# Two paddings move the stationary buffers of an fp32r encoder kernel within 1024 bytes

## The chip, the cores and the metric

The kernel runs on one core of one Trainium2 chip. The metric is the device time of one execution in microseconds (us). Before the change three runs gave 2340.24, 2340.43 and 2341.03 us; the median is 2340.43.

## The reference

One layer of an encoder over 256 tokens of width 2048, in float32. What is computed:

```
x = x + 0.5 * (silu(n1 @ w_gate) * (n1 @ w_up)) @ w_down        # n1 = rms_norm(x), width 5632
h = rms_norm(x);  u = h @ w_in                                  # conv, gate, latents, two merge gates
y_conv = silu(layer_norm(depthwise_conv_31(a * sigmoid(gate)))) @ w_pw_out
y_mla  = attention(16 heads, q from a latent of 768, k and v from a latent of 512, rotary 64) @ w_o
x = x + (sigmoid(gl_conv) * y_conv + sigmoid(gl_mla) * y_mla) @ w_out
x = x + 0.5 * (silu(n2 @ w_gate) * (n2 @ w_up)) @ w_down        # n2 = rms_norm(x), the second feed-forward
return rms_norm(x)
```

All products have float32 operands; the kernel keeps float32 precision by splitting each operand into a high and a low fp32r part and adding three products.

## The kernel before

**Tiling.** The contraction dimension lies on the 128 partitions in tiles of 128 (KT = 16 for width 2048, FT = 44 for 5632, QT = 6, KVT = 4 for the latents). A weight matrix is streamed in units: two contraction tiles of 512 columns each (`DEEP` = 2, `WIDE` = 512), 512 KB. SyncE loads each unit into `raw`, ScalarE rounds it into `w_hi` (L431), VectorE takes the rest into `w_lo` (L926). All three are rings of four slots of 4096 bytes per partition; slot `u % 4` is reused once TensorE has counted unit `u` in `unit_used`.

**TensorE.** `wide_unit` (L770) waits for `lo_ready`, and for both contraction tiles and both halves of the tokens calls `multiply` (L678), which issues three matmuls: at L681 high by high, at L682 high by low, at L683 low by high. So a unit has 12 matmuls. Activations are the stationary operand (128 by 128, loaded by a weight load of its own, PEld in the profile), the streamed weights are the moving one (128 by 512). Which buffer is stationary depends on the stage (`STATIONARY`, L732): `h` for both up/gate stages, conv_in, the latents, the two merge gates and conv_out; `hidden` for both down-projections; `attn` for mla_out; `merged` for w_out; `c_q` for q_rope. In the trace a matmul is named bank<-moving,stationary. The heads (`head_pair`, L833) use products of 256 columns: with the weight block stationary and `c_q` or `c_kv` moving, and for the values with `c_kv` stationary and the weights moving. Scores, probabilities and values are plain float32 matmuls from `q_nope`, `k_nope`, `q_rope`, `probs_t` and `value`.

**Layout of a stationary buffer.** `hidden` is [128, 44, 2, 256] fp32r: per contraction tile 1024 bytes of high parts and 1024 bytes of low parts, each of two halves of 512 bytes (128 tokens). `h`, `attn` and `merged` have the same form with 16 tiles, `c_q` with 6, `c_kv` with 4. A weight slot is 2 x 2048 bytes. So every operand of these matmuls begins a multiple of 512 bytes behind the start of its buffer.

**Places in SBUF.** Buffers are laid one behind the other in the order of their `sb(...)` calls (L172), each rounded up to 32 bytes; members of one `outs` stack share a start. Byte addresses within a partition and their remainders by 1024:

| buffer | address | mod 1024 |
|---|---|---|
| raw, w_hi, w_lo | 1152, 17536, 33920 | 128 |
| x | 50304 | 128 |
| h | 66688 | 128 |
| identity | 99456 | 128 |
| prod (also probs, angle), opened (also probs_t) | 104608, 108704 | 160 |
| before_hidden | 112800 | 160 |
| hidden, padded (they share a start; padded is 18304 bytes) | 112832 | 192 |
| q_rope, attn, merged (they share a start) | 131136 | 64 |
| sig_conv, sig_mla, conv_tok | 163904, 180288, 196672 | 64 |
| c_kv, c_q | 196672, 204864 | 64 |
| k_rope, q_nope, k_nope, value | 217152 to 223296 | 64 |

The last buffer ends at 227392. `before_hidden` is itself a padding that nothing reads or writes.

**Order of the work.** ffn1_up (22 groups of 8 units), ffn1_down (4 groups of 22), conv_in, latents, conv_gate, mla_gate, q_rope, heads, mla_out, conv_out, w_out, ffn2_up, ffn2_down. While conv_in to the heads run, the 31-tap depthwise convolution is made beside them by ScalarE (L539: padded times a tap into q_rope) and VectorE (L1116: sum within q_rope, L1122: padded times a tap plus q_rope). After most groups TensorE turns a result by transposes (L692), which ScalarE (L493) and VectorE (L1058) put into `hidden` or `merged` as high and low parts.

Of the kernel before, what the change touches and what calls it, by code (L numbers as in the profile page):

```python
# [14 lines left out]
P = 128  # L15
# [148 lines left out]
def encoder(nc, streams, xt_in, x_in, pos_in, gains_in, final_in, taps_in, const_in, freq_in, out):  # L164
# [6 lines left out]
    with ExitStack() as ctx:  # L171
        def sb(name, shape, dt=F32, stack=ctx):  # L172
            return stack.enter_context(nc.sbuf_tensor(name, shape, dt))
# [41 lines left out]
        active = prod[:, :, :].rearrange("p a (b t) -> p (a b) t", b=2)  # L215

        sb("before_hidden", [P, 8])

# [9 lines left out]

        padded = sb("padded", [P, KT, T + 2 * PAD])
        conv = padded[:, :, PAD:PAD + T]
        outs = ExitStack()
        attn = sb("attn", [P, KT, 2, T], F32R, outs)
        outs.close()
# [1114 lines left out]
```

## Time and profile before

| | |
|---|---|
| median of three runs | 2340.43 us |
| the profiled execution's own time | 2340.69 us |
| its span, first to last instruction | 2338.9 us |
| TensorE busy | 2312.5 us, 99% |
| VectorE busy | 1322.0 us, 57% |
| ScalarE busy | 1188.5 us, 51% |
| DMA, share of 16 engines | 60.3% |
| granted TensorE clock | 0.998 of full speed |

Matmuls are pipelined, so the length of one in the trace (390 ns for 512 columns) is longer than the distance from its start to the next one's start. Busy time is the union of these spans. What a matmul costs in the stream is read from starts: the start of a late one minus the start of an early one, over the number of steps between them. This distance is called the pitch below. An n-row timeline that shows the first and the last matmul has n - 1 steps.

### The profile page before, as it was taken

To read this page: it belongs to the slowest core of one execution; us is meant where nothing else is said; L and a number is where in the kernel's file an instruction comes from. 1 tells how busy PE (TensorE), PEld (TensorE's weight loads), DVE (VectorE), ACT (ScalarE), POOL (GpSimd) and SP (SyncE) were. 2 spreads that over 40 slices of the span, in tenths; PEclk is the share of its full clock that TensorE was granted. 3 is DMA by queue.
4 is the path that set the end of the run, shared out by engine and by line. 5 is a ranking of instruction groups with operands and counts; after the bars stand their busy time and mean duration, and the time that the engine had idled before them with its cause. 6 is when DMAs were issued, how large, how long until landed. Compare 5 with 4: busy or idle time off the path is not lost.

```text
span 2338.9 us, 26788 instructions
## 1 busy us (share of the span) xinstructions
PE 2312.5 (99%) x10718; PEld 1923.4 (82%) x10718; DVE 1322.0 (57%) x1470; ACT 1188.5 (51%) x1620; POOL 0.2 (0%) x4
## 2 busy tenths in 40 slices
PE   8999999999999999999999999999999999999997
PEld 7888888888888888878889888888888888888886
DVE  5545544544545488997875465555544544544443
ACT  6444444444444577787776564444444444443343
POOL 0000000000000000000000000000000000000000
PEclk9999999999999999999999999999999999999999
DMA  8666666665656666566643456666666666666664
GB/s 287 188 189 192 187 189 191 188 188 188 183 187 183 194 190 183 178 193 186 196 139 116 144 172 188 185 185 207 189 187 191 189 187 192 188 188 189 188 188 128
DMA packets 121532, 432.65 MB, mean 185 GB/s; under 512 B 13632, under 2 KB 13888, under 8 KB 121280
## 3 DMA queue, kind: packets, MB, share of 16 engines
q1 hardware_dynamic: 121408, 430.93, 60.3%
q8 instruction: 85, 1.39, 0.3%
q14 instruction: 39, 0.32, 0.0%
HBM read 428.78 MB, written 2.10 MB: 184 GB/s over the span
## 4 chain that ended last, share of the span: by engine, by line
PE 97%; DVE 1%; ACT 1%; issue 1%; DMA 0%; SPq 0%; ACTq 0%; DVEq 0%
PE bank L681 31%; PE bank L683 31%; PE bank L682 31%; PE turned L692 2%; PE bank L824 1%; PE bank L798 1%; PE bank L799 1%; DVE q_rope L1116 0%; PE turned L809 0%; ACT w_hi L431 0%; DVE w_lo L926 0%; DVE q_rope L1122 0%; DMA raw<-in_ffn_up 0%; PE turned L878 0%; ACT q_rope L539 0%
## 5 line engine op out<-in xcount | busy, mean ns | idle before, releaser
L926 DVE TENSOR_TENSOR w_lo<-raw,w_hi 128x1024 fp32r<-128x1024 f32 (+2 forms) x814 | 986.6, 1215 | 967.8 <-ACT w_hi L431 967.5
L431 ACT ACTIVATE w_hi<-raw 128x1024 fp32r<-128x1024 f32 (+2 forms) x814 | 853.3, 1052 | 1011.4 <-PE bank L683 1004.8
L681 PE MATMUL bank<-w_hi,h 128*128 128x512 f32 (+1 forms) x2144 | 836.0, 390 | 10.3 <-DVE w_lo L926 10.3
L683 PE MATMUL bank<-w_hi,h 128*128 128x512 f32 (+1 forms) x2144 | 832.9, 388 | 0.0
L682 PE MATMUL bank<-w_lo,h 128*128 128x512 f32 (+1 forms) x2144 | 832.8, 388 | 0.0
L681 PEld LDWEIGHTS bank<-w_hi,h 128*128 128x128 f32 x2144 | 403.2, 188 | 93.3 <-DVE w_lo L926 11.6
L683 PEld LDWEIGHTS bank<-w_hi,h 128*128 128x128 f32 x2144 | 403.0, 188 | 82.9
L682 PEld LDWEIGHTS bank<-w_lo,h 128*128 128x128 f32 x2144 | 403.3, 188 | 81.4
L681 PE MATMUL bank<-w_hi,hidden 128*128 128x512 f32 x704 | 278.9, 396 | 0.0
L682 PE MATMUL bank<-w_lo,hidden 128*128 128x512 f32 x704 | 278.4, 395 | 0.0
L683 PE MATMUL bank<-w_hi,hidden 128*128 128x512 f32 x704 | 278.4, 395 | 0.0
L683 PEld LDWEIGHTS bank<-w_hi,hidden 128*128 128x128 f32 x704 | 132.4, 188 | 32.0
L682 PEld LDWEIGHTS bank<-w_lo,hidden 128*128 128x128 f32 x704 | 132.4, 188 | 31.7
L681 PEld LDWEIGHTS bank<-w_hi,hidden 128*128 128x128 f32 x704 | 132.4, 188 | 31.6
L539 ACT ACTIVATE q_rope<-padded,taps 128x256 f32<-128x256 f32 x320 | 135.8, 498 | 1.0 <-DVE q_rope L1116 1.0
L1116 DVE TENSOR_TENSOR q_rope<-q_rope 128x1024 f32<-128x1024 f32 x76 | 92.5, 1217 | 0.0
L1122 DVE SCALAR_TENSOR_TENSOR q_rope<-padded,taps,q_rope 128x256 f32<-128x256 f32 x160 | 66.6, 477 | 0.0
L681 PE MATMUL bank<-w_hi,attn 128*128 128x512 f32 x128 | 52.4, 410 | 0.0
L458 ACT ACTIVATE opened<-bank,rstd 128x512 f32<-128x512 f32 x52 | 33.0, 685 | 37.4 <-PE bank L683 37.4
L681 PE MATMUL bank<-w_hi,merged 128*128 128x512 f32 x128 | 50.6, 395 | 0.0
L683 PE MATMUL bank<-w_hi,merged 128*128 128x512 f32 x128 | 50.2, 392 | 0.0
L683 PE MATMUL bank<-w_hi,attn 128*128 128x512 f32 x128 | 50.2, 392 | 0.0
(171 smaller groups left out, 1219.3 us busy)
## 6 DMA issues: line engine op xcount, KB each, us to landing
raw<-in_ffn_up SPq DMA_DIRECT2D x352, 512.0 KB, 4.0
raw<-in_ffn_down SPq DMA_DIRECT2D x176, 512.0 KB, 3.7
raw<-in_conv_in SPq DMA_DIRECT2D x64, 512.0 KB, 3.8
raw<-in_conv_gate SPq DMA_DIRECT2D x32, 512.0 KB, 4.1
raw<-in_mla_gate SPq DMA_DIRECT2D x32, 512.0 KB, 4.1
raw<-in_mla_out SPq DMA_DIRECT2D x32, 512.0 KB, 3.6
raw<-in_conv_out SPq DMA_DIRECT2D x32, 512.0 KB, 3.6
raw<-in_w_out SPq DMA_DIRECT2D x32, 512.0 KB, 3.6
```

The lines of the kernel that those rows point to most:

```text
L431: act.activation(w_hi[:, j, 0:n], raw[:, j, 0:n], ACT.Copy).then_inc(hi_ready, 1)
L458: act.activation(opened[:, tt, :], banks(g)[tt][:, :], func, scale=rstd[:, tt:tt + 1]).then_inc(by_act, 1)
L539: act.activation(conv_prod[made % 2][:, r, :], padded[:, m, t:t + T], ACT.Copy, scale=taps[:, m, t:t + 1]).then_inc(tap_made, 1)
L681: pe.matmul(dst, fixed_hi, moving_hi, start=first, stop=False)
L682: pe.matmul(dst, fixed_hi, moving_lo, start=False, stop=False)
L683: return pe.matmul(dst, fixed_lo, moving_hi, start=False, stop=last)
L692: last = pe.transpose(turned_bank[n % 2][:, r * T + tt * P:r * T + (tt + 1) * P], src[:, tt, c:c + P], identity[:, :])
L798: pe.matmul(dst, q_nope[:, j, cols], k_nope[:, j, :], start=True, stop=False)
L799: last = pe.matmul(dst, q_rope[:, p, 0, cols], k_rope[:, j, :], start=False, stop=True)
L926: dve.tensor_tensor(w_lo[:, j, 0:n], raw[:, j, 0:n], w_hi[:, j, 0:n], ALU.subtract).then_inc(lo_ready, 1)
L1116: dve.tensor_tensor(dst, conv_acc, conv_prod[made % 2], ALU.add).then_inc(tap_done, 1)
L1122: dve.scalar_tensor_tensor(out=conv_acc[:, r, :], in0=padded[:, m, t:t + T], scalar=taps[:, m, t:t + 1], in1=conv_acc[:, r, :], op0=ALU.mu ...
```

## The change

`before_hidden` grows from 8 to 248 float32 values per partition (32 to 992 bytes), and a new padding `before_attn` of 32 values (128 bytes) is put between `padded` and the buffers that begin with `attn`, `q_rope` and `merged`. Neither is read or written. No instruction, wait, size, shape or order of the kernel changes.

```diff
@@ -215,7 +215,7 @@
-        sb("before_hidden", [P, 8])
+        sb("before_hidden", [P, 248])
@@ -231,6 +231,7 @@
         padded = sb("padded", [P, KT, T + 2 * PAD])
         conv = padded[:, :, PAD:PAD + T]
+        sb("before_attn", [P, 32])
         outs = ExitStack()
         attn = sb("attn", [P, KT, 2, T], F32R, outs)
```

By the rule above `hidden`, `padded`, `xt`, `x0_squares` and `final_gain` move up by 960 bytes, and `attn`, `q_rope`, `merged` and all that lies behind them by 960 + 128 = 1088 bytes. `hidden` then begins at 113792 (128 mod 1024), `attn` and `merged` at 132224 (128), `c_kv` at 197760 (128), `c_q` at 205952 (128). The last buffer ends at 228480.

## Rows read from the trace of the kernel before

**Rows 1.** The page: busy us of each engine; the granted clock in tenths.

```profile
PE 2312.5 (99%) x10718; PEld 1923.4 (82%) x10718; DVE 1322.0 (57%) x1470; ACT 1188.5 (51%) x1620; POOL 0.2 (0%) x4
...
PEclk9999999999999999999999999999999999999999
```

**Rows 2.** The page: the chain that ended last, by engine.

```profile
PE 97%; DVE 1%; ACT 1%; issue 1%; DMA 0%; SPq 0%; ACTq 0%; DVEq 0%
```

**Rows 3.** Timeline of PE: start us, length us, operation; stationary h, 90 rows.

```profile
1139.67 0.39 PE L682 MATMUL bank<-w_lo,h 128*128 128x512 f32 x1
...
1159.84 0.39 PE L681 MATMUL bank<-w_hi,h 128*128 128x512 f32 x1
```

**Rows 4.** Timeline of PE, the second down-projection, 86 rows.

```profile
2119.98 0.39 PE L682 MATMUL bank<-w_lo,hidden 128*128 128x512 f32 x1
...
2139.81 0.40 PE L683 MATMUL bank<-w_hi,hidden 128*128 128x512 f32 x1
```

**Rows 5.** Timeline of PE, w_out with stationary merged, 49 rows.

```profile
1532.90 0.39 PE L681 MATMUL bank<-w_hi,merged 128*128 128x512 f32 x1
...
1543.88 0.39 PE L681 MATMUL bank<-w_hi,merged 128*128 128x512 f32 x1
```

**Rows 6.** Timeline of PE, q_rope stage with stationary c_q, 50 rows.

```profile
1165.75 0.39 PE L683 MATMUL bank<-w_hi,c_q 128*128 128x512 f32 x1
...
1176.96 0.39 PE L681 MATMUL bank<-w_hi,c_q 128*128 128x512 f32 x1
```

**Rows 7.** Groups of PE by form: count, busy us, mean ns, idle before.

```profile
L682 PE MATMUL bank<-w_lo,hidden 128*128 128x512 f32 x704 | 278.4, 395 | 0.0
...
L682 PE MATMUL bank<-w_lo,merged 128*128 128x512 f32 x128 | 49.8, 389 | 0.0
L682 PE MATMUL bank<-w_lo,attn 128*128 128x512 f32 x128 | 49.8, 389 | 0.0
...
L682 PE MATMUL bank<-w_lo,c_q 128*128 128x512 f32 x24 | 9.4, 393 | 0.0
```

**Rows 8.** Timeline of DVE during the first down-projection, 17 rows.

```profile
515.17 1.23 DVE L926 TENSOR_TENSOR w_lo<-raw,w_hi 128x1024 fp32r<-128x1024 f32 x1 [1.57 <-ACT w_hi L431]
...
559.97 1.23 DVE L926 TENSOR_TENSOR w_lo<-raw,w_hi 128x1024 fp32r<-128x1024 f32 x1 [1.57 <-ACT w_hi L431]
```

**Rows 9.** Groups of PE by form: short products of the heads.

```profile
L682 PE MATMUL bank<-c_q,w_hi 128*128 128x256 f32 x96 | 26.8, 279 | 0.0
...
L682 PE MATMUL bank<-c_kv,w_hi 128*128 128x256 f32 x64 | 18.0, 281 | 0.0
```

**Rows 10.** Timeline of PE, heads, c_kv moving, then stationary, 24 rows.

```profile
1219.93 0.28 PE L682 MATMUL bank<-c_kv,w_hi 128*128 128x256 f32 x1
...
1222.65 0.28 PE L681 MATMUL bank<-w_hi,c_kv 128*128 128x256 f32 x1
```

**Rows 11.** Timeline of PE, heads, c_q moving, 12 rows.

```profile
1245.60 0.28 PE L683 MATMUL bank<-c_q,w_lo 128*128 128x256 f32 x1
...
1246.85 0.28 PE L682 MATMUL bank<-c_q,w_hi 128*128 128x256 f32 x1
```

**Rows 12.** Timeline of PE, 320 columns with stationary h, 18 rows.

```profile
971.98 0.30 PE L681 MATMUL bank<-w_hi,h 128*128 128x320 f32 x1
...
974.47 0.31 PE L683 MATMUL bank<-w_hi,h 128*128 128x320 f32 x1
```

**Rows 13.** Groups of DVE, 820:1070: count, busy us, mean ns, idle before, releaser.

```profile
L926 DVE TENSOR_TENSOR w_lo<-raw,w_hi 128x1024 fp32r<-128x1024 f32 (+1 forms) x93 | 109.6, 1185 | 30.7 <-ACT w_hi L431 30.6
L1116 DVE TENSOR_TENSOR q_rope<-q_rope 128x1024 f32<-128x1024 f32 x49 | 59.6, 1217 | 0.0
L1122 DVE SCALAR_TENSOR_TENSOR q_rope<-padded,taps,q_rope 128x256 f32<-128x256 f32 x103 | 42.9, 477 | 0.0
```

**Rows 14.** Waits: engine and line, releaser, us in total, times, longest.

```profile
ACT w_hi L431 <- PE bank L683: 1004.8, 635, 2.2
...
PE bank L681 <- DVE w_lo L926: 10.3, 4, 8.4
```

## The prediction

> **What bounds the kernel now.** I read the page first: TensorE is busy 99% of the span at full granted clock in every slice [rows 1], and the chain that ended last is TensorE for 97% [rows 2]. The waits say the same from the other side: ScalarE waits 1004.8 us in all for TensorE to give back a ring slot, while TensorE waits 10.3 us for weights [rows 14]. So only two things can move the time: the number of matmuls, which the change leaves alone, and what one costs in the stream. The engines that feed it have room.
>
> That cost is read next, from starts in the timeline, stage by stage. With stationary `h`: 90 rows from 1139.67 to 1159.84, so 20.17 us over 89 steps = 226.6 ns a matmul [rows 3]. With stationary `hidden`: 86 rows, 19.83 us over 85 steps = 233.3 ns [rows 4]. The first down-projection has the same pitch, seen from VectorE, which splits one unit of weights per 12 matmuls: 44.80 us over 16 steps = 2.800 us, and 2.800 / 12 = 233.3 ns [rows 8]. With stationary `merged`: 10.98 us over 48 steps = 228.8 ns [rows 5]. With stationary `c_q`: 11.21 us over 49 steps = 228.8 ns [rows 6]. These are the same 512 columns, the same moving buffers and the same three-product pattern; 512 columns at 2.4 GHz, the granted level, are 213.3 ns, so `h` pays 13.3 ns on top, `merged` and `c_q` 15.5, `hidden` 20.0.
>
> **What the difference goes with.** By the table of places, `w_hi`, `w_lo` and `h` stand at 128 in 1024 bytes; `merged` and `c_q` at 64; `hidden` at 192. Equal place has the lowest pitch; two buffers at 64 have one pitch though they lie 73 KB apart. I tried three other readings against this. It is not how far up in SBUF the buffer lies: `hidden` covers 112832 to 202944, which contains `merged`, and `c_q` lies above it all, yet both are cheaper. It is not the neighbours' work: VectorE is idle 1.57 us of each 2.80 us unit in the down-projection [rows 8], and in the w_out stage the other engines do the same weight work. It is not a wait, because a wait would show as a few long steps, and here the whole stream is slower. What the trace can't separate is place relative to the weights from place as such; after the change both are those of `h`, so the forecast does not need it. The chunks within a buffer begin at multiples of 512 bytes in all of them, so nothing within it spoils the equality. What the equality does not cover are the remainders by 4096 and more; within `h` these run through all values while the pitch stays 226.6, so I take them as without effect.
>
> A rule speaks against the change. The Trainium skill, "TensorE: Matmul & The Clock Gate", in the section on what happens when you issue a matmul, says that TensorE has two independent read ports, so that loading the next weights does not take read bandwidth from the running matmul; it gives 215.7 ns as the distance of warm matmuls of 512 columns. By it no place could matter and the gain would be nil. This case's trace disagrees on the level already: 226.6 to 233.3 ns, at the full clock.
>
> **The change, part by part.** Nothing is added to any queue; no instruction, wait or transfer is moved past another. Only addresses change.
>
> *hidden, 192 to 128.* Three lines of 704 matmuls are 2112 [rows 7]. Each goes from 233.3 to 226.6 ns [rows 3, 4]: 2112 x 6.66 ns = 14.1 us, all on the path, since TensorE is the chain there.
>
> *attn and merged, 64 to 128.* Three lines of 128 for each are 768 [rows 7]. `merged` goes from 228.8 to 226.6 ns [rows 3, 5]; `attn` begins at the same address, and I take its pitch as that of `merged`: 768 x 2.12 ns = 1.6 us.
>
> *c_q as the stationary buffer, 64 to 128.* Three lines of 24 are 72 [rows 7]: 72 x 2.15 ns = 0.2 us [rows 3, 6].
>
> *The short products of the heads.* Here `c_q` moves (3 x 96 products) and `c_kv` moves or is stationary (3 x 64 each way), 672 in all [rows 9], with 256 columns. Before no row shows them at equal place. Their pitch now has two levels: 2.72 us over 23 steps = 118.3 ns [rows 10] and 1.25 us over 11 steps = 113.6 ns [rows 11]. Lower bound of the new cost: all at 113.6 ns, a gain of at most 672 x 4.7 ns = 3.2 us. Upper bound: a short product at equal place is shown with 320 columns and stationary `h`, 2.49 us over 17 steps = 146.5 ns [rows 12]; 320 columns at 2.4 GHz are 133.3 ns, so it pays 13.2 ns, as the long ones do. Carried to 256 columns (106.7 ns) that is 119.9 ns, a loss of at most 672 x 6.3 ns = 4.2 us. The rows nearest in shape are the heads' own, between the two ends; I take 0, and keep -3.2 and +4.2.
>
> *Plain float32 products and transposes* read buffers that also move. They show no effect of place that I can price, and I take 0.
>
> *The other engines.* `padded` and `q_rope`, on which the convolution runs, both come to 128. The sum within `q_rope` takes 1217 ns, all its operands being at one place already [rows 13]; so equal places are no burden to VectorE there. 0, with the far end priced as a rival.
>
> *What is late next.* A unit of the down-projections shrinks from 2.80 to 12 x 226.6 ns = 2.72 us. That is the rate at which ScalarE, VectorE and the loads already feed the `h` stages. VectorE's idle time per unit falls from 1.57 to 1.49 us. If that cover were absent, the 14.1 us would be lost in part, which is the same result as the partial rival below.
>
> Sum: 14.1 + 1.6 + 0.2 + 0 = 15.9 us. Against the profiled execution's own 2340.69 us this is 2324.8; the median of the three runs is 0.26 us lower, so the forecast is 2340.4 - 15.9 = **2324.5 us**, 0.7% less.
>
> **The rivals.**
>
> *A: only part of it goes away.* `hidden` differs from `h` also in its depth of 44 tiles and in the remainders by larger powers of two. If it falls only to the 228.8 ns that `merged` and `c_q` have, and they stay, the gain is 2112 x 4.5 ns = 9.6 us: 2330.8 us. For it: these are the only other values seen. Against it: the pitch is flat in both down-projections, whatever the tile [rows 4, 8].
>
> *B: place is not the cause*, and the paddings do nothing, by the rule of ports or because the stage sets the pitch in a way I haven't seen: 2340.4 us. For it: in the trace place and buffer always go together, so this is a correlation over four buffers. Against it: `merged` and `c_q`, in different stages and of different depth, agree to 0.1 ns.
>
> *C: slower, through the convolution.* Now that `padded`, `q_rope` and the rings share one place, VectorE's tap operations could clash. In 820 to 1070 us they are 59.6 + 42.9 = 102.5 us, and VectorE is idle for 30.7 us [rows 13]. Longer by a share g they cost 102.5g - 30.7 once that is positive. To end 4.7 us above the time before, with the 15.9 us saved, 102.5g has to be 51.3, so it decides from g = 0.5 on. At a doubling it is 71.8 us: 2340.4 - 15.9 + 71.8 = 2396.3 us. Against it: 1217 ns within `q_rope`, at one place, beside 1185 ns for the split, at one place too [rows 13].
>
> **How the numbers follow.** Forecast 0.81, A 0.08, B 0.08, C 0.03. The forecast's own range is 2324.5 - 3.2 = 2321.3 to 2324.5 + 4.2 = 2328.7. The range given reaches on to A and leaves out B and C: 2321 to 2332. What a measurement of this kernel can tell from no change is about 0.2%, 4.7 us; so faster is the forecast and A, 0.89; the same is B, 0.08; slower is C, 0.03.
>
> **What would show it.** In the changed kernel's timeline the down-projections must have 226.6 ns from start to start and VectorE's splits there a period of 2.72 us; the two down-projections together must be 14 us shorter, half in each. `merged`, `attn` and `c_q` must read 226.6. The `h` stages must not change. The heads tell the open term: 113.6, 118.3 or 119.9 ns. If `hidden` reads 228.8, A holds; if it reads 233.3, B does. If the tap operations are longer than 1217 and 477 ns, C is at work. The prediction would be wrong above all if equal place were good only together with something else that `h` has and `hidden` has not.

## The result and the profile after

The changed kernel took 2326.68 us (median of six runs, 2326.39 to 2327.34) against 2340.67 us for the kernel before beside it: a ratio of 0.9941 with a 95% interval of 0.9929 to 0.9953, or 14.0 us less. The forecast was 15.9 us less; the time lies inside its range of 2321 to 2332 us.

The page of the changed kernel, to be read against [rows 1]:

```profile
span 2324.8 us, 26788 instructions
...
PE 2299.0 (99%) x10718; PEld 1924.4 (83%) x10718; DVE 1322.2 (57%) x1470; ACT 1188.3 (51%) x1620; POOL 0.2 (0%) x4
...
PEclk9999999999999999999999999999999999999999
```

TensorE is busy 99% of the span at full clock as before, with the same 10718 matmuls; its busy time fell by 13.5 us and the span by 14.1. So the matmuls themselves became cheaper. The timeline of TensorE in the second down-projection, the same stretch as [rows 4], first and last of 88 rows:

```profile
2119.96 0.39 PE L683 MATMUL bank<-w_lo,hidden 128*128 128x512 f32 x1
...
2139.68 0.39 PE L683 MATMUL bank<-w_lo,hidden 128*128 128x512 f32 x1
```

19.72 us over 87 steps are 226.7 ns, where 233.3 ns stood before. VectorE's splits in the first down-projection (first and last of 17 rows), against [rows 8]:

```profile
514.10 1.23 DVE L927 TENSOR_TENSOR w_lo<-raw,w_hi 128x1024 fp32r<-128x1024 f32 x1 [1.49 <-ACT w_hi L432]
...
557.62 1.23 DVE L927 TENSOR_TENSOR w_lo<-raw,w_hi 128x1024 fp32r<-128x1024 f32 x1 [1.49 <-ACT w_hi L432]
```

43.52 us over 16 steps are 2.72 us a unit, or 226.7 ns for each of 12 matmuls. The heads show the other sign. A run of their short products, first and last of 17 rows, against [rows 10] and [rows 11]:

```profile
1214.03 0.28 PE L683 MATMUL bank<-w_lo,c_kv 128*128 128x256 f32 x1
...
1215.95 0.29 PE L684 MATMUL bank<-w_hi,c_kv 128*128 128x256 f32 x1
```

1.92 us over 16 steps are 120.0 ns, where 118.3 and 113.6 ns stood in [rows 10] and [rows 11]. Over all steps with `c_q` or `c_kv` (under 200 ns, 628 of them) the mean went from 116.8 to 119.8 ns.

The stages, from the first start to the last one of one line (columns: count, least, median and greatest length in ns, first and last start in us). The kernel before: the two down-projections, the first product of the heads, `attn`, `merged`:

```profile
L681 PE MATMUL bank<-w_hi,hidden x352: 393/398/481, 499.0 to 748.1; 128*128 128x512 f32 x176
...
L681 PE MATMUL bank<-w_hi,hidden x352: 393/396/476, 2078.3 to 2324.8; 128*128 128x512 f32 x176
...
L681 PE MATMUL bank<-c_q,w_hi x96: 276/281/469, 1182.0 to 1298.6; 128*128 128x256 f32 x96
...
L681 PE MATMUL bank<-w_hi,attn x128: 392/394/584, 1308.7 to 1407.7; 128*128 128x512 f32 x128
...
L681 PE MATMUL bank<-w_hi,merged x128: 388/394/477, 1498.2 to 1588.9; 128*128 128x512 f32 x128
```

The changed kernel (L682 is L681 of before, since a line was added above it):

```profile
L682 PE MATMUL bank<-w_hi,hidden x352: 389/389/477, 498.2 to 740.5; 128*128 128x512 f32 x176
...
L682 PE MATMUL bank<-w_hi,hidden x352: 389/389/477, 2071.2 to 2310.8; 128*128 128x512 f32 x176
...
L682 PE MATMUL bank<-c_q,w_hi x96: 277/283/472, 1174.3 to 1292.5; 128*128 128x256 f32 x96
...
L682 PE MATMUL bank<-w_hi,attn x128: 387/389/586, 1302.7 to 1401.4; 128*128 128x512 f32 x128
...
L682 PE MATMUL bank<-w_hi,merged x128: 389/389/476, 1491.9 to 1581.9; 128*128 128x512 f32 x128
```

| stretch | before, us | after, us | difference | forecast |
|---|---|---|---|---|
| first down-projection | 249.1 | 242.3 | -6.8 | -7.0 |
| second down-projection | 246.5 | 239.6 | -6.9 | -7.0 |
| heads | 116.6 | 118.2 | +1.6 | 0 (-3.2 to +4.2) |
| attn | 99.0 | 98.7 | -0.3 | -0.8 |
| merged | 90.7 | 90.0 | -0.7 | -0.8 |

The rows sum to -13.1 us. Of the rest of the span's 14.1 us, 0.8 us had passed already when `hidden` began (499.0 against 498.2 in these rows), in a stage that the change does not touch. That is scatter from run to run: in the twelve profiles in which `h` lies at equal place, `hidden` begins anywhere between 497.8 and 499.3 us. So that much is not credited to the change. (`c_q` as the stationary buffer, not in the table, took 17.13 us from its first to its last start before and 17.00 after.)

### The profile page after: what moved, and what is told of

It reads as the page before. It is cut to its first block, busy times and chain, and to the rows that moved or that the text cites. A ratio compares the mean times of both kernels' runs of the same rounds, so it can differ in the third digit from the quotient of the medians.

```text
span 2324.8 us, 26788 instructions
## 1 busy us (share of the span) xinstructions
PE 2299.0 (99%) x10718; PEld 1924.4 (83%) x10718; DVE 1322.2 (57%) x1470; ACT 1188.3 (51%) x1620; POOL 0.2 (0%) x4
## 4 chain that ended last, share of the span: by engine, by line
PE 97%; DVE 1%; ACT 1%; issue 1%; DMA 0%; SPq 0%; ACTq 0%; DVEq 0%
PE bank L682 31%; PE bank L684 31%; PE bank L683 31%; PE turned L693 2%; PE bank L825 1%; PE bank L799 1%; PE bank L800 1%; DVE q_rope L1117 0%; PE turned L810 0%; ACT w_hi L432 0%; DVE w_lo L927 0%; DVE q_rope L1123 0%; DMA raw<-in_ffn_up 0%; PE turned L879 0%; ACT q_rope L540 0%
## 5 line engine op out<-in xcount | busy, mean ns | idle before, releaser
L682 PE MATMUL bank<-w_hi,h 128*128 128x512 f32 (+1 forms) x2144 | 835.9, 390 | 10.1 <-DVE w_lo L927 10.1
L684 PE MATMUL bank<-w_hi,h 128*128 128x512 f32 (+1 forms) x2144 | 832.7, 388 | 0.0
L682 PEld LDWEIGHTS bank<-w_hi,h 128*128 128x128 f32 x2144 | 403.0, 188 | 92.7 <-DVE w_lo L927 11.4
L684 PEld LDWEIGHTS bank<-w_hi,h 128*128 128x128 f32 x2144 | 402.9, 188 | 83.1
L682 PE MATMUL bank<-w_hi,hidden 128*128 128x512 f32 x704 | 274.3, 390 | 0.0
L684 PE MATMUL bank<-w_hi,hidden 128*128 128x512 f32 x704 | 273.9, 389 | 0.0
L684 PEld LDWEIGHTS bank<-w_hi,hidden 128*128 128x128 f32 x704 | 132.1, 188 | 27.5
L682 PEld LDWEIGHTS bank<-w_hi,hidden 128*128 128x128 f32 x704 | 132.1, 188 | 27.4
L1117 DVE TENSOR_TENSOR q_rope<-q_rope 128x1024 f32<-128x1024 f32 x76 | 92.6, 1218 | 0.0
L682 PE MATMUL bank<-w_hi,attn 128*128 128x512 f32 x128 | 52.0, 407 | 0.0
L682 PE MATMUL bank<-w_hi,merged 128*128 128x512 f32 x128 | 50.2, 392 | 0.0
L684 PE MATMUL bank<-w_hi,attn 128*128 128x512 f32 x128 | 50.1, 392 | 0.0
L683 PE MATMUL bank<-w_lo,attn 128*128 128x512 f32 x128 | 49.9, 390 | 0.0
```

What stands on the lines that cost most here:

```text
L682: pe.matmul(dst, fixed_hi, moving_hi, start=first, stop=False)
L683: pe.matmul(dst, fixed_hi, moving_lo, start=False, stop=False)
L684: return pe.matmul(dst, fixed_lo, moving_hi, start=False, stop=last)
L1117: dve.tensor_tensor(dst, conv_acc, conv_prod[made % 2], ALU.add).then_inc(tap_done, 1)
```

## The experiments

All but `e6_hidden_16` differ from the kernel before by paddings alone. A distance below is the place of the stationary buffer less that of the moving one; for products of 512 columns the moving one is a weight ring. As `s1` and the runs behind it show, it counts by its remainder by 256, so 192 means 64 bytes short. To follow the addresses one thing in the rule for places has to be put right: buffers of different `outs` stacks share a start, and those of one stack lie one behind the other, as `probs` and `probs_t` do in the table.

**Each part alone.** `e1_hidden_only` moves `hidden` and puts the buffers behind it back to 64:

```diff
-        sb("before_hidden", [P, 8])
+        sb("before_hidden", [P, 248])
+        sb("before_attn", [P, 16])
```

> Only the feed-forward's buffer moves: hidden to 128 in 1024 bytes, while attn, merged, c_kv and c_q stay at 64. Theory (a buffer's place against the weight rings sets the pitch, and nothing else does): hidden reads 226.6 ns from start to start, merged and c_q stay at 228.8, the short products of the heads stay at 113.6 to 118.3 ns, and the time is 2340.7 - 14.1 = 2326.6 us, the same as with both paddings, since what those lose on attn, merged and c_q here the heads give back. Rival (moving the heads' buffers cost nothing, and hidden brought only the 12.3 us that are left of 14.0 after attn, merged and c_q): 2328.4 us.

Measured: 2326.87 us (2326.63 to 2328.67, five runs), ratio 0.9944 (0.9932 to 0.9957). All steps with stationary `hidden` have a mean of 226.7 ns, those with `merged` and `c_q` 228.9. The first product of the heads in its tile view:

```profile
L682 PE MATMUL bank<-c_q,w_hi x96: 276/281/470, 1175.0 to 1291.6; 128*128 128x256 f32 x96
```

1291.6 - 1175.0 = 116.6 us, the value of before. The forecast's term for `hidden` and the loss in the heads are both as the theory has them. The rival's 2328.4 us is not met by the median, though one of the five runs took 2328.67; what decides against it is that the heads fell back by the 1.6 us. Moving `attn`, `merged`, `c_kv` and `c_q` brought nothing on balance.

`e2_heads_back` keeps both paddings and takes the heads' buffers out of equal place again, together with all that lies behind `merged`:

```diff
+        sb("before_sig_conv", [P, 112])
         sig_conv = sb("sig_conv", [P, 2, D])
```

> Both paddings stay, and a third of 448 bytes ahead of sig_conv puts c_kv and c_q at 576 in 1024, which is 64 in 512. Theory (the place counts by its remainder by 512, since every operand begins a multiple of 512 bytes behind its buffer's start): the short products fall back from 120 ns to the 113.6 to 118.3 of before, the heads take the 126.8 us of before and not 128.4, c_q as the stationary buffer reads 228.8, and the time is 2326.7 - 1.6 + 0.2 = 2325.3 us. Rival (the remainder by 1024 counts, so 576 is a new place): the short products read something else than either. Second rival (the 1.6 us more in the heads are not from their place): 128.4 us and 2326.8 us.

Measured: 2325.08 us (2324.53 to 2326.11), ratio 0.9935 (0.9921 to 0.9948). Its heads:

```profile
L683 PE MATMUL bank<-c_q,w_hi x96: 276/281/469, 1175.1 to 1291.9; 128*128 128x256 f32 x96
```

1291.9 - 1175.1 = 116.8 us, against 118.2 in the changed kernel. (The 126.8 and 128.4 us of the expectation run on to the first product of `attn`.) `c_q` as the stationary buffer reads 228.9 ns, and the mean of the short products is 117.1. So what the heads had lost came from the place of `c_kv` and `c_q`, and a place 512 bytes further on is the same place. The padding moves the operands of the plain float32 products too, but those kept their 215.8 ns. To see whether this version is really ahead of the changed kernel, both ran on one chip, as `e7_change_again` and `e8_heads_back_again`.

> The changed kernel itself once more, beside the next one on one chip: 2326.7 us.

> The changed kernel with the third padding, which puts c_kv and c_q at 64 in 512 again, beside the changed kernel on one chip. Theory (equal place is dearer for products of 256 columns, cheaper for 512): 1.4 to 1.6 us below the changed kernel, 2325.1 us against 2326.7. Rival (the 1.6 us between the two earlier results came from the chip or the hour): no difference between these two.

Measured: 2326.52 us (2326.16 to 2327.08, five runs) for the changed kernel and 2325.36 us (2324.81 to 2325.83, five runs) for the one with the third padding. The two sets of runs do not touch; the difference is 1.2 us, somewhat under the 1.4 to 1.6 expected. Their ratios to the kernel before, 0.9940 and 0.9935, have intervals that overlap widely (0.9926 to 0.9954 and 0.9921 to 0.9949), so the ratios alone would not tell them apart. The version with the third padding has the shortest time here.

**Distance or place.** `e3_all_64` shifts all buffers together, the rings and the stationary ones among them:

```diff
+        sb("before_raw", [P, 16])
         raw = sb("raw", [P, SLOTS, UNIT])
-        sb("before_hidden", [P, 8])
+        sb("before_hidden", [P, 248])
+        sb("before_attn", [P, 32])
```

> Both paddings, and one more of 64 bytes ahead of raw: rings, h, hidden, attn, merged, c_kv and c_q all stand at 192 in 1024, equal among each other. Theory (distance between the stationary buffer and the rings counts): every long product stays at 226.6 ns, the short ones at 120, the time is the 2326.7 us of both paddings. Rival (the place 128, a multiple of 128 bytes, is what is good, whatever the rings have): the long products read 228.8 to 233.3 ns or more, over 9312 of them 20 us or more on top: 2347 us or longer.

Measured: 2326.49 us (2326.18 to 2327.41, four runs), ratio 0.9942 (0.9928 to 0.9955). Second down-projection, first and last of 88 rows:

```profile
2119.96 0.39 PE L683 MATMUL bank<-w_hi,hidden 128*128 128x512 f32 x1
...
2139.68 0.39 PE L683 MATMUL bank<-w_hi,hidden 128*128 128x512 f32 x1
```

226.7 ns, though `hidden` stands at 192 in 1024 again, where it was at 233.3 ns before. What changed is that the rings stand there too. The place as such is out for this pair of places; the distance is what counts. The prediction had left this open.

`e5_h_64` asks the same of `h`, which the change left alone (`identity`, `prod`, `opened` and the small buffers between `h` and `before_hidden` move 64 bytes with it):

```diff
+        sb("before_h", [P, 16])
         h = sb("h", [P, KT, 2, T], F32R)
-        sb("before_hidden", [P, 8])
+        sb("before_hidden", [P, 232])
+        sb("before_attn", [P, 32])
```

> Both paddings, but h, which the change did not move, is put 64 bytes further than the rings, and all behind it stays where it was. Theory (distance sets the pitch for any buffer): the h stages go from 226.7 to 233.3 ns, as hidden had at that distance: 6336 x 6.6 ns = 41.8 us, and the 96 products of 320 columns add at most 1 us: 2368.5 to 2369.5 us. Rival (h is quick for another reason, its 16 tiles or the low part of SBUF): 2326.7 us.

Measured: 2367.88 us (2367.53 to 2368.24, two runs), ratio 1.0118 (1.0089 to 1.0148). Second up stage, first and last of 45 rows:

```profile
1739.66 0.39 PE L683 MATMUL bank<-w_hi,h 128*128 128x512 f32 x1
...
1749.93 0.39 PE L685 MATMUL bank<-w_hi,h 128*128 128x512 f32 x1
```

10.27 us over 44 steps are 233.4 ns. The same distance gives the same pitch in another buffer with 16 tiles and low in SBUF, and the size follows: 41.2 us over the 2326.68 us, where 41.8 were expected for the 512-column products alone, so the time is 0.6 us below the expected range. The 96 products of 320 columns kept 146.6 ns, as in the changed kernel. Their second tile begins 1280 bytes into a weight slot, which is a multiple of 256 and not of 512; the layout section's multiples of 512 hold for the other products only.

**Other distances.** `s1`, `n1`, `n2` and `n3` put each buffer at its own distance, so one profile gives several points. Each ran once, so the distances are read from steps and not from the time. Their edits are four paddings, in values of 4 bytes (a dash means that there is no such padding; the kernel before has only the first one, with 8):

```
          before_hidden   before_attn   before_sig_conv   before_c_q
s1             56              -             232               8
n1             48             48              24              56
n2              -             16              48              32
n3             32             16              32              48
```

> A first look at other distances from the rings (at 128): hidden at 384 (256 further), attn and merged at 256 (128 further), c_kv at 160 (32 further), c_q at 192 (64 further). 
Measured, `s1`: 2330.16 us. `hidden` 256 bytes away, first and last of 89 rows:

```profile
2119.82 0.39 PE L683 MATMUL bank<-w_hi,hidden 128*128 128x512 f32 x1
...
2139.77 0.39 PE L684 MATMUL bank<-w_lo,hidden 128*128 128x512 f32 x1
```

19.95 us over 88 steps are 226.7 ns: the value of equal place to the tenth, and not the clear difference that was expected. `merged`, 128 bytes away, first and last of 48 rows:

```profile
1532.95 0.39 PE L684 MATMUL bank<-w_lo,merged 128*128 128x512 f32 x1
...
1543.86 0.40 PE L683 MATMUL bank<-w_hi,merged 128*128 128x512 f32 x1
```

10.91 us over 47 steps are 232.1 ns (232.4 over all its 375 steps under 300 ns). `c_q`, now 64 further, has a mean of 233.3 ns over its 69 steps under 300 ns, where it had 228.9 at 64 short: so 64 on one side and 64 on the other differ, and the rival of hidden's own properties falls.

> The look before showed hidden 256 bytes from the rings at the same 226.7 ns as at 0, so distances count by their remainder by 256: 0 gives 226.7, 64 gives 233.3, 128 gives 232.4, 192 gives 228.9 ns. Here hidden is at 224, attn and merged at 32, c_kv at 128, c_q at 96. Theory (a smooth curve with its bottom at equal place): hidden about 227.8, merged about 230, c_q as stationary about 233, total about 2340.4 - 2112 x 5.5 ns + 768 x 1.2 ns = 2329.7 us. Rival (the bottom lies beside equal place, at 224): hidden below 226.6, time below 2328.5 us, and then h, with 6336 matmuls, should be moved too.

Measured, `n1`: 2345.6 us, beside 2341.86 (one run) for the kernel before. `hidden` at 224: 86 rows, 19.83 us over 85 steps, 233.3 ns. `merged` at 32: 48 rows, 10.96 us over 47 steps, 233.2 ns. Both theories missed.

> hidden at 32, attn and merged at 224, c_kv at 160, c_q at 32 bytes from the rings, by 256. Theory (smooth, bottom at equal place): hidden about 230, merged about 227.8, total about 2340.4 - 2112 x 3.3 ns - 768 x 1.0 ns = 2332.7 us. Rival (the bottom is on this side, at 32): hidden below 226.6 ns. The short products of the heads read other values than 120 ns at both places, as they did at every distance but 0.

Measured, `n2`: 2343.91 us beside 2341.86. `hidden` at 32, first and last of 86 rows:

```profile
2119.95 0.40 PE L686 MATMUL bank<-w_hi,hidden 128*128 128x512 f32 x1
...
2139.78 0.40 PE L684 MATMUL bank<-w_hi,hidden 128*128 128x512 f32 x1
```

233.3 ns again. `merged` at 224: 47 rows, 10.74 us over 46 steps, 233.5 ns. The short products did read below 120 ns with `c_q`, at 117.0, but with `c_kv` as the stationary buffer they read 120.0.

> hidden at 160, attn and merged at 96, c_kv at 224, c_q at 160 bytes from the rings, by 256. Theory (smooth): hidden about 231, halfway from 232.4 to 228.9; merged about 233; total about 2340.4 - 2112 x 2.3 ns + 768 x 4 ns = 2338.6 us. Rival (the pitch has narrow dips, by 32-byte steps): any of them at or below 226.6 ns.

Measured, `n3`: 2344.62 us beside 2341.86. `hidden` at 160: 233.3 ns (19.83 us over 85 steps). `merged` at 96, first and last of 47 rows:

```profile
1532.95 0.40 PE L685 MATMUL bank<-w_lo,merged 128*128 128x512 f32 x1
...
1543.72 0.39 PE L686 MATMUL bank<-w_hi,merged 128*128 128x512 f32 x1
```

10.77 us over 46 steps are 234.1 ns, the highest seen. All three missed in time by 6 to 16 us for one reason: the curve is not smooth.

| distance by 256, bytes | 0 | 32 | 64 | 96 | 128 | 160 | 192 | 224 |
|---|---|---|---|---|---|---|---|---|
| pitch, 512 columns, ns | 226.7 | 233.3 | 233.3 | 234.1 | 232.1 | 233.3 | 228.8 | 233.3 |
| pitch, 256 columns, ns | 119.5 to 120.0 | 118.2 to 118.3 | 115.9 to 117.8 | 118.3 to 118.8 | 118.3 to 118.8 | 119.9 to 120.0 | 117.0 to 117.9 | 116.7 to 117.1 |

In the row of 512 columns there is one narrow dip at equal place, a second, shallower one at 192, where `merged` and `c_q` stood before, and nothing lower at these steps. What the change could bring to the long products was brought by reaching 0. That the remainder by 256 is what counts rests on more than `s1`: `hidden` at 32 (`n2`) and `merged` at 288 (`n1`) both have a mean of 233.3 ns, `merged` at 96 (`n3`) and `c_q` at 608 (`n1`) both 234.2, `hidden` at 160 and `c_q` at 416 (`n3`) 233.3 and 233.4.

The row of 256 columns holds the means of the heads' products over the kernel before, the changed one, `e1` to `e3`, `s1` and `n1` to `n3`. Here too the distance is stationary less moving, so where `c_q` or `c_kv` moves it is the weights' place less theirs: in `n2` one and the same `c_kv`, 160 bytes past the rings' place, read 120.0 ns as the stationary buffer (distance 160) and 118.3 as the moving one (distance 96), and `c_q` moving at distance 160 (`n1`) read 119.9. Equal place is the dearest for these products, but 160 is as dear.

**How narrow.** `e6_hidden_16` goes to a distance that paddings can't make:

```diff
-        hidden = sb("hidden", [P, FT, 2, T], F32R, outs)
+        hidden_and_4 = sb("hidden", [P, FT * 2 * T + 4], F32R, outs)
+        hidden = hidden_and_4[:, 4:FT * 2 * T + 4].rearrange("p (k s t) -> p k s t", k=FT, s=2)
```

> Both paddings, and hidden begins 16 bytes (four values) further, a distance from the rings that the paddings, which come in 32 bytes, can't make. Theory (a narrow dip at equal place, as 32 bytes further already cost the full 6.6 ns): hidden reads between 226.7 and 233.3 ns; at 233.3 the time is 2326.7 + 14.0 = 2340.7 us. Rival (the bottom of the dip lies a few values beside equal place): hidden below 226.6 ns and a time below 2326.5 us.

Measured: 2330.37 us (one run). Two stretches of the same down-projection, the first with 178 rows, the second with 87:

```profile
519.71 0.39 PE L685 MATMUL bank<-w_hi,hidden 128*128 128x512 f32 x1
...
559.83 0.39 PE L685 MATMUL bank<-w_hi,hidden 128*128 128x512 f32 x1
```

```profile
599.76 0.40 PE L685 MATMUL bank<-w_hi,hidden 128*128 128x512 f32 x1
...
619.83 0.39 PE L684 MATMUL bank<-w_lo,hidden 128*128 128x512 f32 x1
```

40.12 us over 177 steps are 226.7 ns; 20.07 us over 86 steps are 233.4 ns. The same instructions on the same buffers run at either pitch. No stretch between two groups of transposes lies in between: those of the first down-projection read 226.7, 233.3, 233.3 and 226.7 ns. The timeline where it first changes:

```profile
564.36 0.39 PE L684 MATMUL bank<-w_lo,hidden 128*128 128x512 f32 x1
564.59 0.39 PE L685 MATMUL bank<-w_hi,hidden 128*128 128x512 f32 x1
564.82 1.03 PE L694 MATMUL turned<-identity,x 128*128 128x128 f32 x8
565.61 0.48 PE L683 MATMUL bank<-w_hi,hidden 128*128 128x512 f32 x1
565.92 0.40 PE L684 MATMUL bank<-w_lo,hidden 128*128 128x512 f32 x1
566.16 0.40 PE L685 MATMUL bank<-w_hi,hidden 128*128 128x512 f32 x1
```

Until then a step is 0.23 us and the average 226.7. Eight transposes pass, and behind them the stream stays in the dearer rhythm, through another group of transposes at 627 us; where transposes pass at 689.75 us, it falls back. The whole second down-projection kept 226.7 ns. So the pitch is a rhythm that the stream of matmuls and weight loads settles into. At equal place it was the cheap one in every long stretch (`hidden` 226.7 to 226.8 ns in all of them in the changed kernel), at 16 bytes either can hold, at 32 bytes it is the dear one.

**Which operand.** `e4_wlo_64` moves one ring by 64 bytes (`x` goes with it; `h` and all behind it move by 256, which is no move for the distance):

```diff
+        sb("before_w_lo", [P, 16])
         w_lo = sb("w_lo", [P, SLOTS, UNIT], F32R)
+        sb("before_h", [P, 48])
         h = sb("h", [P, KT, 2, T], F32R)
```

(and the two paddings of the change)

> Both paddings, and w_lo alone 64 bytes further (two more paddings keep h, hidden, attn, merged, c_kv and c_q at equal place with w_hi). Theory (the moving operand of a matmul and the weights loaded for the next one must stand at equal place): only the step from the matmul that moves w_lo, the second of the three, to the third gets longer, by 2.2 to 6.7 ns as the distance of 64 costs; the steps behind the two that move w_hi stay at 226.7. 3104 long steps x 2.2 to 6.7 ns: 2326.7 + 7 to 21 = 2334 to 2347 us. Rival (the place of w_hi or of raw against the stationary buffer counts, since ScalarE and VectorE read there): no step changes, 2326.7 us.

Measured: 2372.48 us (one run), 45.8 more than the changed kernel, outside both. Seven matmuls in a row in the second down-projection (L684 and L686 move `w_hi`, L685 moves `w_lo`):

```profile
2129.75 0.40 PE L684 MATMUL bank<-w_hi,hidden 128*128 128x512 f32 x1
2129.98 0.40 PE L685 MATMUL bank<-w_lo,hidden 128*128 128x512 f32 x1
2130.21 0.39 PE L686 MATMUL bank<-w_hi,hidden 128*128 128x512 f32 x1
2130.44 0.40 PE L684 MATMUL bank<-w_hi,hidden 128*128 128x512 f32 x1
2130.68 0.39 PE L685 MATMUL bank<-w_lo,hidden 128*128 128x512 f32 x1
2130.91 0.39 PE L686 MATMUL bank<-w_hi,hidden 128*128 128x512 f32 x1
2131.14 0.40 PE L684 MATMUL bank<-w_hi,hidden 128*128 128x512 f32 x1
```

Here all three lines have steps of 0.23 to 0.24 us, and their means over all steps with stationary `hidden` are 231.4 (L684), 232.2 (L685) and 232.4 ns (L686), each from some 700 steps under 300 ns. Two of the three still move a ring at equal place, and they are as dear as the third. The rival is out, as `w_lo`'s place does count; my theory that each step pays for its own pair is out too. One matmul in three out of place is enough to make all three dearer; the products of 256 columns became cheaper by it, 117.9 ns against 119.8. What e4 leaves open is also whether the distance of `w_lo` from the stationary buffer counts or that from `w_hi`, as both changed. With what e6 showed the loss of a common rhythm fits, but which meeting of which reads makes the rhythm was not measured: no run separated the weight load's read from the moving operand's.

## Why the prediction was right, point by point

- *hidden, 14.1 us.* Right. 233.3 went to 226.7 ns in both halves; the stages are 13.7 us shorter between the starts shown, and `e1_hidden_only` confirms it with all behind `hidden` at its old remainder by 1024.
- *attn and merged, 1.6 us.* `merged` has its 0.7 of 0.8 us. `attn` gave 0.3 of 0.8. I had taken its pitch as that of `merged` since both begin at one address, without a row of its own. Its four longer stretches (24 to 96 products, 188 steps) did go down, from 43.63 to 43.26 us, 1.9 ns a step beside the 2.12 forecast. Its other 16 stretches are of 12 products between two groups of transposes, and those gained nothing: 41.85 us over 176 steps before, 41.96 after. One of them before and the same one after, first and last of 12 rows:

```profile
1342.48 0.48 PE L681 MATMUL bank<-w_hi,attn 128*128 128x512 f32 x1
...
1345.09 0.39 PE L683 MATMUL bank<-w_hi,attn 128*128 128x512 f32 x1
```

```profile
1336.36 0.47 PE L682 MATMUL bank<-w_hi,attn 128*128 128x512 f32 x1
...
1338.96 0.40 PE L684 MATMUL bank<-w_hi,attn 128*128 128x512 f32 x1
```

From first to last start they take 2.61 and 2.60 us. In the changed kernel the first step behind a group of transposes takes 313 ns or more, the next five to nine go up and down between 224 and 236 ns before they come to 226 and 227, and then the stretch is nearly over. In the kernel before the steps went round 226, 229 and 232 ns, 228.9 in the mean, and were there sooner. So the forecast's price holds only for a stream that has settled.
- *c_q as the stationary buffer, 0.2 us.* Right: 228.9 went to 227.0 ns, which is 0.1 us.
- *The short products of the heads, 0 in a range of -3.2 to +4.2 us.* This is the term that was mis-sized: it measured +1.6 us between the starts shown. The upper bound had it right to the tenth of a nanosecond, 119.9 ns forecast and 120.0 measured: at equal place a matmul pays 13.3 ns on top of its columns at each of the three widths, 226.7 for 512, 146.6 for 320, 120.0 for 256. I took the heads' own rows as nearest in shape. The nearest in the thing that was changed, the distance, was the row with 320 columns. The price at the upper end was still too large, 4.2 us, as it was worked out from the cheaper of the two levels seen before for all 672 products; from the dearer one, 1.7 ns each, it would have been 1.1 us, and from the mean over all steps before, 116.8 ns, 672 x 3.0 = 2.0 us.
- *The other engines, 0.* Right. The convolution's operations on VectorE in 820 to 1070 us, against [rows 13]:

```profile
L1117 DVE TENSOR_TENSOR q_rope<-q_rope 128x1024 f32<-128x1024 f32 x50 | 60.9, 1218 | 0.0
L1123 DVE SCALAR_TENSOR_TENSOR q_rope<-padded,taps,q_rope 128x256 f32<-128x256 f32 x101 | 42.1, 479 | 0.0
```

1218 and 479 ns, where 1217 and 477 stood, and rival C is out.

- *What is late next, nothing.* Right: VectorE waits 1.49 us a unit in the down-projection, as worked out.
- *Rival A* (228.8 ns) did not come. That value belongs to the distance 192 and not to a part of the cause. *Rival B*, and with it the rule of the Trainium skill in "TensorE: Matmul & The Clock Gate", section on what happens when you issue a matmul, that the weight load's read port leaves the running matmul alone: the runs speak against its consequence here. Moving `h` by 64 bytes against the rings moved its pitch by 6.7 ns (e5), moving both together did not (e3), and even the best is 226.7 ns and not the 215.7 that the page gives.

The sum therefore reads 13.7 + 0.7 + 0.3 + 0.1 - 1.6 = 13.2 us in the stages, 14.0 in the medians, against 15.9 forecast. No two errors hid each other: the heads (1.6 us) and `attn` (0.5) both made the gain smaller than the sum. The main step of the prediction rested on a correlation over four buffers, as it said itself; a rule of place as such would have given the same time, and only `e3_all_64` and `e5_h_64` tell the two apart.

## What to carry to other kernels

Where TensorE is the bound and its stream has no gaps, read the pitch per stationary buffer from starts in the timeline and set it beside each buffer's address less that of the moving one: two pitches for the same shape are a hint that costs a padding to follow. Put both at equal remainders by 256 bytes for products of 512 columns, move all rings together, and check the shorter products separately: here 256 columns were better off 64 bytes out of equal place, by 1.2 us in this kernel. Short stretches between transposes gained nothing here, so count only the stretches that are longer. When a shape has no row at the new setting, take the row that shares the setting, not the one that shares the shape.

## What the runs showed of the hardware

- The start-to-start time of fp32r matmuls of 512 columns with a weight load before each depends on the distance between the stationary and the moving buffer (stationary less moving), by its remainder by 256 bytes: 226.7 ns at 0, 228.8 at 192, 232 to 234 elsewhere at steps of 32 bytes. With 256 columns it is 120.0 ns at 0 and at 160, and 115.9 to 118.8 elsewhere.
- It is a rhythm with memory. At 16 bytes the same stream ran at 226.7 and at 233.4 ns, changing at transposes (564.82 and 689.75 us in e6). Behind a group of transposes it takes up to nine steps of 224 to 236 ns to settle at equal place, so stretches of 12 products did not gain (41.85 us before, 41.96 after). With one of two moving buffers 64 bytes off, all three steps went to 231 to 232 ns.
- At equal place the addition is 13.3 ns at 256, 320 and 512 columns: 120.0, 146.6 and 226.7 ns lie on one line of 0.417 ns a column, which is 2.4 GHz. Out of it the addition varied with the width: 15.5 to 20.8 ns with 512 columns, but 6.9 to 11.6 ns with 256 in [rows 10] and [rows 11] and up to 13.3 at 160; with 320 columns, 64 bytes off, e5 and the changed kernel have one mean, 146.6 ns, over 95 steps each.
- Plain float32 products of 256 columns kept 215.8 ns a pass in both kernels. For `q_nope` with `k_nope` and `q_rope` with `k_rope` the distance was 0 in both, so that says nothing of distance; for `value` with `probs_t` it went from 160 to 224, and the pass from 215.5 to 215.9 ns. The convolution's operations on VectorE kept their lengths to 2 ns.
